# A two-layer hybrid decoder on one core: the order of work ahead of the first projections

## The reference, cut to what matters

```python
def rmsnorm(x, g):
    y = xf * lax.rsqrt(jnp.mean(xf * xf, axis=-1, keepdims=True) + EPS)
    return (y * g.astype(jnp.float32)).astype(x.dtype)

def even_mixer(h, cos, sin, w_in, conv_w, q_g, k_g, w_out):
    p = h @ w_in
    sc, q, k, v, iq, ik, iw = jnp.split(p, EVEN_SPLIT, axis=-1)
    ...
    q = apply_partial_rope(rmsnorm(q...), cos, sin)
...
x = x + even_mixer(rmsnorm(x, ev_norm[i]), cos, sin, ev_w_in[i], ...)
```

## Time and profile before

| | |
|---|---|
| median of 3 runs | 2174.93 us |
| the profiled execution: its own time | 2174.65 us |
| its span | 2172.9 us, 29914 instructions |
| mean granted TensorE clock | 0.98 |
| PE busy | 2066.8 us (95%) |
| DVE busy | 1396.7 us (64%) |
| ACT, POOL busy | 1101.1 us, 1101.0 us (51% each) |

### The profile page before, as it was taken

How to read it: one execution, slowest core, us unless ns; L and a number is a source line. 1 busy time by engine, 2 the same in 40 slices (tenths; PEclk the granted TensorE clock), 3 DMA queues, 4 the chain that set the end, 5 groups by cost and what they waited for, 6 DMA issues and landing times. The chain is left out here.

```text
span 2172.9 us, 29914 instructions
## 1 busy us (share of the span) xinstructions
PE 2066.8 (95%) x11334; PEld 1005.1 (46%) x11334; DVE 1396.7 (64%) x1998; ACT 1101.1 (51%) x1648; POOL 1101.0 (51%) x841
## 2 busy tenths in 40 slices
PE   6989977789999999999999999989999999999998
PEld 3544435654444444444444444555444444444444
DVE  8778888866775575575555036695867467467552
ACT  6459946644664564555423224443566456455520
POOL 6104323315576766766585013503476766765742
PEclk8999988999999999999999999999999999999999
DMA  4001110002111211212142001101211211211212
GB/s 175 20 1 49 41 31 2 13 13 71 49 58 53 65 53 55 63 54 59 51 121 68 0 20 40 41 10 51 57 49 51 67 59 47 70 58 50 59 41 96
DMA packets 186493, 110.20 MB, mean 51 GB/s; under 512 B 4351, under 2 KB 180902, under 8 KB 186358
## 3 DMA queue, kind: packets, MB, share of 16 engines
q1 hardware_dynamic: 185894, 107.00, 16.5%
q0 software_dynamic: 464, 1.39, 0.2%
HBM read 104.18 MB, written 4.19 MB: 50 GB/s over the span
## 5 line engine op out<-in xcount | busy, mean ns | idle before, releaser
L1229 PE MATMUL ps<-arena 128*128 128x512 f16 x2712 | 593.9, 379 | 3.9 <-DVE ps L2749 2.6
L1229 PEld LDWEIGHTS ps<-arena 128*128 128x128 f16 x2712 | 264.7, 98 | 325.9 <-DVE ps L2749 5.5
L1229 PE MATMUL ps<-h_hi,arena 128*128 128x512 f16 x1216 | 370.9, 380 | 5.1 <-DVE arena L2840 4.5
L782 POOL TENSOR_SCALAR w_scaled<-stage 128x1024 f32<-128x1024 f32 (+4 forms) x82 | 79.9, 974 | 578.7 <-PE ps L1088 414.6
L2758 DVE SCALAR_TENSOR_TENSOR work<-ps,fvec,work 128x1023 f32<-128x1023 f32 (+1 forms) x176 | 221.7, 1279 | 21.9 <-ACT work L1966 18.8
L1229 PE MATMUL ps<-h_lo,arena 128*128 128x512 f16 x608 | 231.0, 380 | 0.0
L1229 PEld LDWEIGHTS ps<-h_hi,arena 128*128 128x128 f16 x1216 | 119.2, 98 | 151.6 <-issue 7.5
L1088 PE MATMUL ps<-arena 128*128 128x512 f16 x708 | 156.4, 383 | 14.0 <-DVE xT L2640 11.7
L836 POOL TENSOR_TENSOR w_scaled<-stage 128x512 f32<-128x512 f32 (+2 forms) x62 | 70.0, 1128 | 193.4 <-ACT stage L1697 193.1
L1697 ACT ACTIVATE stage<-stage 128x2048 f32<-128x2048 f32 (+2 forms) x62 | 104.7, 1688 | 111.8 <-DMA stage<-in_ffn_w_up_dram 96.0
L1088 PE MATMUL ps<-h_hi,arena 128*128 128x512 f16 x576 | 150.0, 381 | 3.2 <-ACT small L1869 1.7
(11 more groups left out here) (370 smaller groups left out, 3865.9 us busy)
## 6 DMA issues: line engine op xcount, KB each, us to landing
stage<-in_ffn_w_up_dram SPq DMA_DIRECT2D x84, 512.0 KB, 3.8
stage<-in_ffn_w_down_dram SPq DMA_DIRECT2D x48, 384.0 KB, 3.2
stage<-in_od_w_in_dram SPq DMA_DIRECT2D x20, 512.0 KB, 3.8
stage<-in_ev_w_in_dram SPq DMA_DIRECT2D x12, 512.0 KB, 3.7
arena<-in_x_dram SPq DMA_DIRECT2D x8, 512.0 KB, 6.9
stage<-in_ffn_w_down_dram SPq DMA_DIRECT2D x16, 256.0 KB, 2.7
out_dram<-arena SPq DMA_DIRECT2D x8, 512.0 KB, 3.5
stage<-in_od_w_out_dram SPq DMA_DIRECT2D x12, 256.0 KB, 2.8
```

The lines of the kernel that those rows point to most:

```text
L782: nc.gpsimd.tensor_scalar(scaled, src, W_SCALE, 1.0, ALU.mult, ALU.mult).then_inc(w_parts, 1)
L1229: last = mm(ps[:, bank, :], left, b[:, k, :], start=(fresh and k == 0 and pss == 0), stop=(k == nk - 1 and pss == 2), skip_group_check=True)
```

## The change

**Order of loads.** x blocks 0 to 3, the six vectors, x blocks 4 to 7. **Norm by token.** ACT squares a block and takes its root at once (the Sqrt table is loaded at the start by a dummy), DVE takes the reciprocal after copying that block out, and POOL multiplies the block in `x_tok` in place by it (`normalise(b)`, blocks 0 to 3 in the middle of the 19 angle steps, 4 to 7 behind them). **Second turn.** PE turns the normed tokens again, 4 transposes to a piece (`h_turn(m)`, banks 4 to 7), and ACT and DVE make h_hi and h_lo right out of PSUM, with the gain in the same instruction. `spread(0, ...)`, DVE's f32 products of norm 0 and their buffers go. **Two blocks together.** For each k PE does hi x hi and lo x hi of blocks 0 and 1 (8 matmuls) and then `h_turn(4 + k)`; after all k come the products with the low weights, block 0 with `h_turn(12)` to `h_turn(15)` between, then block 1. **Gaps.** DVE makes the low parts of weight tiles 0 to 4, POOL of 5 to 7; two mask levels go behind the norm; the sines go between pieces 11 and 12; `conv_vectors` goes behind `tm_lo(0)`.

```diff
-        TW_BY_DVE = (0, 1)
-        TW_BY_POOL = (2, 3, 4, 5, 6, 7)
+        TW_BY_DVE = (0, 1, 2, 3, 4)
+        TW_BY_POOL = (5, 6, 7)
...
+            for b in range(NB // 2):
+                load_x(b)
...
+            for b in range(NB // 2, NB):
+                load_x(b)
...
+            def normalise(b):
+                pool.wait_ge(x_turned, 2 * b + 2)
+                pool.wait_ge(tok_rstd, b + 1)
+                G.tensor_scalar(x_tok[:, b, :], x_tok[:, b, :], rms8[:, b:b + 1], 1.0, ALU.mult, ALU.mult).then_inc(tok_normed, 1)
...
             for src, dst in ((2, 4), (3, 5)):
+                if src == 3:
+                    for b in range(NB // 2):
+                        normalise(b)
...
+            for b in range(NB // 2, NB):
+                normalise(b)
...
+            def h_turn(m):
+                hf, k = divmod(m, KT)
+                if k == 0:
+                    pe.wait_ge(tok_normed, 4 * hf + 4)
...
+                if m >= 4:
+                    pe.wait_ge(h_ready, m - 3)
+                for j in range(4):
+                    last = tr(ps[:, 4 + m % 4, j * P:(j + 1) * P], x_tok[:, 4 * hf + j, k * P:(k + 1) * P], ident[:])
+                last.then_inc(hf_ready, 1)
+
+            for b in range(6):
+                x_turn(b)
...
+            x_turn(6)
+            h_turn(0)
+            h_turn(1)
+            h_turn(2)
+            x_turn(7)
+            h_turn(3)
...
-            spread(0, 0)
-            spread(0, 1)
...
-            tm_project(0)
+            pe.wait_ge(x_evict, 2 * NB)
+            for k in range(KT):
+                pe.wait_ge(tw_hi_made, k + 1)
+                wait_tile(0, 0, k)
+                for b in range(2):
+                    for a in (h_hi, h_lo):
+                        for c0, c1 in ((0, HALF), (HALF, EV_TM)):
+                            mm(pair(b)[:, c0:c1], a[:, k, b * P:(b + 1) * P], tw_hi[:, k, c0:c1], start=(k == 0 and a is h_hi), stop=False)
+                h_turn(4 + k)
+            for b in range(2):
+                for k in range(KT):
...
+                    for c0, c1 in ((0, HALF), (HALF, EV_TM)):
+                        last = mm(pair(b)[:, c0:c1], h_hi[:, k, b * P:(b + 1) * P], tw_lo[:, k, c0:c1], start=False, stop=(k == KT - 1))
+                    if b == 0 and k % 2:
+                        h_turn(12 + k // 2)
+                last.then_inc(tm_done, 1)
...
-            tm_project(1)
             tm_project(2)
...
+                A(work[:, b % 2, :], x_tok[:, b, :], ACT.Square, accum_out=rms8[:, b:b + 1]).then_inc(sq_ready, 1)
+                act.wait_ge(sq_ready, b + 1)
+                A(rms8[:, b:b + 1], rms8[:, b:b + 1], ACT.Sqrt, bias=eps[:, 0:1], scale=1.0 / D).then_inc(tok_rms, 1)
...
+                for b in range(6):
+                    square_tokens(b)
...
+                square_tokens(6)
...
+                first_high(0)
+                for k in range(KT):
                     tw_high(k)
-                for m in range(2 * KT):
-                    high(0, m)
-                    if m + 3 < KT:
-                        tw_high(m + 3)
+                    if k + 1 < KT:
+                        first_high(k + 1)
+                    if k == 1:
+                        square_tokens(7)
...
+            first_low(0)
+            first_low(1)
+            for m in range(2, KT):
+                first_low(m)
+                if m == 2:
+                    token_root(NB - 1)
+                if m - 2 in TW_BY_DVE:
+                    tw_low(m - 2)
+            for m in range(KT, 2 * KT):
+                first_low(m)
+            level_masks(5, LEVELS + 1)
...
             for b in range(NB):
+                if b == 1:
+                    conv_vectors()
                 tm_sum(b)
-                if b == 0:
-                    conv_vectors()
```

More of the change, by code:

```diff
@@ L146, in build @@
         vrows = view(8192, [P])
-        frows = work[:, 1, 0:4 * P].rearrange("p (q m) -> p q m", m=P)
+        frows = work[:, 3, 0:4 * P].rearrange("p (q m) -> p q m", m=P)
         q_st = view(0, [HEADS, T], F16)
@@ L611, in _, with load_x @@
             sp.dma_start(pos_i[0:NB, :], t["positions"].rearrange("a (b p) -> (a b) p", p=P)).then_inc(pos_landed, 16)
-            for b in range(NB):
+            def load_x(b):
                 sp.dma_start(x_tok[:, b, :], t["x"][0, b * P:(b + 1) * P, :]).then_inc(x_landed[b], 16)
+            for b in range(NB // 2):
+                load_x(b)
             def load(src, slot, dst):
@@ L1015, in _, with x_turn @@
             tr(ps[:, 6, 0:NB], pos_f[0:NB, :], ident[0:NB, 0:NB]).then_inc(pos_turned, 1)
-            for b in range(NB):
+            def x_turn(b):
                 pe.wait_ge(x_landed[b], 16)
@@ L1683, in after_register_wait, with square_tokens @@
                 act.sem_inc(act_passed, 1)
+            act.wait_ge(dve_filled, 3)
+            A(small[:, 62:63], eps[:, 0:1], ACT.Sqrt)
             act.wait_ge(pos_turned, 1)
             A(ang[:, 0, 0:NB], ps[:, 6, 0:NB], ACT.Copy).then_inc(rope_act, 1)
-            for b in range(NB):
+            def square_tokens(b):
                 act.wait_ge(x_landed[b], 16)
@@ L2307, in root, with norm @@
             def root(n, hf):
-                dve.wait_ge(rms_ready, 2 * n + hf)
+                dve.wait_ge(rms_ready, NB + 2 * n + hf - 1)
                 V.reciprocal(rms8[:, 4 * hf:4 * hf + 4], rms8[:, 4 * hf:4 * hf + 4]).then_inc(rstd_ready, 1)
-            def norm(n, gain, name=None, pairs=None):
-                if n == 0:
-                    dve.wait_ge(rms_ready, 1)
-                    V.reciprocal(rms8[:], rms8[:]).then_inc(rstd_ready, 1)
-                    for k in TW_BY_DVE:
-                        tw_low(k)
-                    dve.wait_ge(vec_ready, 1)
-                else:
-                    add_tile_half(name, pairs[0], 0, 0)
-                    add_square_half(n, 0, 0)
-                    add_tile_half(name, pairs[1], 1, 0)
-                    add_square_half(n, 1, 0)
-                    root(n, 0)
-                    add_tile_half(name, pairs[0], 0, 1)
+            def norm(n, gain, name, pairs):
+                add_tile_half(name, pairs[0], 0, 0)
+                add_square_half(n, 0, 0)
+                add_tile_half(name, pairs[1], 1, 0)
+                add_square_half(n, 1, 0)
+                root(n, 0)
+                add_tile_half(name, pairs[0], 0, 1)
                 def low(m):
@@ L2345, in norm @@
                     if k == 0:
[L2346 removed]
+                        dve.wait_ge(rstd_spread, NB + 2 * n + hf - 1)
                     if m >= 4 and n % 2 == 0:
@@ L2351, in norm @@
                                            op1=ALU.mult).then_inc(hf_ready, 1)
-                    if n and m == 0:
+                    if m == 0:
                         add_square_half(n, 0, 1)
-                    if m >= 1 and (n == 0 or m != KT):
+                    if m >= 1 and m != KT:
                         low(m - 1)
-                    if n and m == 3:
+                    if m == 3:
                         add_tile_half(name, pairs[1], 1, 1)
-                    if n and m == 4:
+                    if m == 4:
                         add_square_half(n, 1, 1)
-                    if n and m == 6:
+                    if m == 6:
                         root(n, 1)
-                    if n and m == KT - 1:
+                    if m == KT - 1:
                         low(m)
@@ L2369, in _ @@
             dve.wait_ge(dve_filled, 4)
+            for b in range(NB):
+                x_out(b)
+                if b < NB - 1:
+                    token_root(b)
+            first_low(0)
+            first_low(1)
+            for m in range(2, KT):
+                first_low(m)
+                if m == 2:
+                    token_root(NB - 1)
[4 more added lines that the diff above has]
+            level_masks(5, LEVELS + 1)
             dve.wait_ge(x_evict, 2 * NB)
-            norm(0, VEC_AT["ev_norm"])
             dve.wait_ge(tw_split_dve, len(TW_BY_DVE))
```

84 lines of the change are left out of this document (52 added, 32 removed).

## The result

| | before | after |
|---|---|---|
| median of the runs | 2175.24 us (2174.39 to 2176.79, 4 runs) | 2163.05 us (2159.09 to 2166.98, 4 runs) |
| the profiled execution: own time, span | 2174.65, 2172.9 us | 2161.33, 2159.6 us |
| granted TensorE clock, mean | 0.98 | 0.986 |
| instructions | 29914 | 30031 |
| `tm_turn(0)` starts at | 65.30 us | 55.11 us |

The ratio is 0.9944 (0.9933 to 0.9956): faster by 0.4% to 0.7%. The sum of the prediction said 9.5 us up to `tm_turn(0)`, and the trace shows 10.2 there.

What follows compares the result with a forecast made beforehand. PE was taken as the bound from 44.7 to 124.9 us, with losses before it in a late first product and waits for POOL. Saving 65.3 - 55.8 = 9.5 us at `tm_turn(0)` gave 2165.4 us, range 2162.8 to 2170.8.

Steps and rivals of the forecast that it cites:

- The start: From the landing of x to PE's first product: PE starts at 18.1 us instead of 23.53.
- near end of the bounds: POOL's norm of one token block takes 1.13 us; the far end was 3.70.
- rival 1: PE's clock falls in its gap at 17 us: 2.5 us lost, 2167.9 us; chance 0.18.
- The joint pass: Projection of blocks 0 and 1 together: 2.15 us a tile, 17.2 for eight; with block 2, done at 55.2.
- 0.8 us that I allowed for a late DVE: In the projection of blocks 0 and 1: DVE late once with its supplies, 0.8 us, between 0 and 3.
- tm_turn(0): PE's turn after block 2: starts at 55.8 against 55.2, a wait of 0.6 us, ends 0 and 3.5.
- rival 2: At `tm_turn(0)` DVE's last block 0 instructions queue behind POOL's: a wait of 3 us, 2167.8 us; chance 0.11.
- at most 1 us of wait: Sign in the profile: `tm_turn(0)` at 55 to 57 us with at most 1 us of wait.
- Every later stage of the same length: Behind `tm_turn(0)`: every later stage keeps its length and comes 9.5 us earlier.
- noise term of 0.7 us: Noise of the runs, 0.7 us, counted in the best case of 2162.8 us.
- rival 4: The clock stays at the lower level while transposes are mixed in: turn at 75.4, 2185 us; chance 0.03.
- Rival 3: POOL norms at the slow rate, 3.70 us each, PE starting at 27.0: 3.3 slower, 2178.2 us; chance 0.08.

Runs made afterwards that it cites:

- slow_norm: Changed kernel with POOL's norm as multiply, then maximum with -3.0e38, instead of multiply, multiply; same values. Median 2179.98 us, 1.002 of the kernel before.
- pool_waits: Changed kernel with POOL waiting for the low parts of projection block 0 before splitting the next weights' first two units. Median 2165.38 us, 0.9958 of the kernel before.
- again: The changed kernel run once more with nothing edited, also called the repeat. Median 2166.23 us, 0.9959 of the kernel before.
- warm: Changed kernel plus 30 unread f32 identity transposes on PE in its wait before `index_head(5, 0)`. Median 2165.26 us, 0.995 of the kernel before.
- before_dve3: Kernel before the change, with DVE making low parts of weight tiles 0 to 2, POOL 3 to 7. Median 2175.97 us, 0.9998 of the kernel before.
- lows_by_pool: Changed kernel with low parts of weight tiles shared as before: DVE 0 and 1, POOL 2 to 7. Median 2169.0 us, 0.9966 of the kernel before.
- blocks_apart: Changed kernel with the joint pass undone: block 0 with all three passes per tile, then block 1. Median 2173.65 us, 0.9992 of the kernel before.

## Why the prediction was right

**The start** (predicted 18.1, measured 18.21). The near end of the bounds, 1.13 us a norm, was the right one; slow_norm shows that the other end belongs to its pair of operations. POOL's second four end at 22.4, and nobody waits for them. A token block takes ACT 1.37 us with its root; I had 1.5. PE idles 1.26 us before its first product (1.1 predicted) and the clock stays at 1.00 until 119.4, so rival 1 did not happen.

**The joint pass** (predicted 2.15 a tile, measured 2.07). Eight matmuls were right at 1.63; a turn takes 0.44 behind matmuls, not the 0.5 taken from sixteen in a row. The 0.8 us that I allowed for a late DVE did not come: its low parts of weights take 1.28 to 1.41 and one 2.54, but PE never waits. The turning of `frows` takes 0.30 (43.04 to 43.34), where I had 0.6. Block 2 starts at 43.34 instead of 44.5, and PE reaches `tm_turn(0)` at 53.3, 1.9 us ahead of my 55.2.

**tm_turn(0)** (predicted 55.8 with a wait of 0.6, measured 55.11 with 1.80). This term was mis-sized by 1.2, inside its ends of 0 and 3.5. The mechanism was the one named, and rival 2's: DVE's last instructions of block 0 behind POOL's splits. I had them end at 55.8 and they end at 55.05. The two sizes hide each other: PE came 1.9 us early and could use 0.7 of it. That is why the saving is 10.2 instead of 9.5, and that the two came out so close is in part luck. The sign "at most 1 us of wait" failed; the turn's time didn't. In parts: 5.3 at the start (23.53 to 18.21), 6.5 from there to block 2 (31.63 us before, 25.13 after), less 1.6 for the wait that came instead.

On the last two instructions of that chain a rule bears that the trace supports. DVE's subtraction of 256 columns takes 0.42 us in pool_waits and 1.25 in after, and the only difference is POOL's work beside it; its instructions that read one operand from PSUM keep 0.74 (`h_lo`, L2358: 0.74 to 0.75 for all sixteen, eleven of them while POOL is busy between 17 and 35 us). The Trainium skill (SBUF — State Buffer, SBUF: two separate sides) says that an operation of VectorE with two SBUF inputs and one of GpSimd that reads SBUF lock each other out of a shared pair of ports for a whole instruction; the trace agrees.

**"Every later stage of the same length"** is the step that failed. The part behind the turn was 3.1 us shorter than before's in the first trace and 0.7 shorter in the repeat, and what differs comes and goes with the clock: behind 128 us in the trace of before, and at 318 to 400, 1143 to 1434 and 1988 to 2000 us between the two traces of the changed kernel. The forecast of 2165.4 lies between the medians of after (2163.05) and again (2166.23); the first of them has two runs below the range's low end, 2162.8, and the noise term of 0.7 us that I gave it was too small. The ranges of the changed kernels in the table are 3 to 9 us wide. The range's high end, 2170.8, doesn't come out of the terms that it names: either of the first rivals with DVE late by 2 more gives 2169.8 or 2169.9.

**The clock and the transposes** (rival 4). The clock is 1.00 through the 25 us in which transposes and matmuls alternate. Ahead of them PE has had nothing but transposes since 2.7 us, and in the trace of after their clock is the full one from 10.2 us on:

```profile
10.20:17.00 6.80, 6.76 (x59) 6.14 (x57) 6.70 (x17) 6.67 (x17) 5.46 (x11) 1.00 1.03 417
```

By the Trainium skill (TensorE: Matmul & The Clock Gate, Part 4: PE-mode transpose) the full clock should not engage for them; the trace contradicts it here, as the rows of before already did.

**Rival 3** did not happen and was priced well: 2178.2 against 2179.98 measured once POOL was made slow. The sign of the whole change hung on the second operation of one instruction.

## What to carry to other kernels

Where an engine whose clock can fall waits for supplies, look first for work of its own that needs fewer supplies and put that ahead: here waits of 2.69 and 4.55 us cost PE 1.9 and 1.5 us of clock on top. Before you shorten a chain, look for a second one of the same length at its end, as DVE's was at `tm_turn(0)`; and when you move the work that disturbs it, put it where the disturbed engine idles, not just behind the place where it hurt. In a kernel whose clock moves by itself, compare the time of the same instruction in two traces, since the end time can't tell 2 us, and take off what they already differ by where their work is still the same. And before you credit an edit with having kept the clock up, look whether it also stays up in a trace without the edit.

## What the runs showed of the hardware

- POOL's one-input instruction takes 1.12 us for 1024 columns with (multiply, multiply) and a factor from memory, and 3.7 with (multiply, maximum) on the same operands (slow_norm).
- A DVE instruction on two operands in SBUF takes up to 2.57 us beside POOL: 2.14 for 40 columns (before_dve3), 2.16 for 80 and 2.57 for 576 (pool_waits), where undisturbed ones take 0.19 to 0.76. Its own size hardly matters.
- Executions of one kernel differ by up to 9.4 us (warm). In the two traces of the changed kernel the differing stages are those where the granted clock differs, and the stretches of lower clock are not at the same places in two executions of the same kernel.
- The length of one wait doesn't tell whether PE's clock falls. The first matmuls ran at the lower of the two clocks after waits of 2.69 (lows_by_pool) and 4.55 us (blocks_apart), and at the higher after 1.26, 1.80 and 2.07 us. But after 3.25 us in slow_norm and 3.46 us in lows_by_pool and pool_waits they ran at the higher too, and in before after 2.07 us at the lower:

```profile
38.32 1.76 PE L1542 MATMUL ps<-arena,h_hi 128*128 128x512 f16 x4 [2.07 <-POOL arena L945]
```
